# FFN output projection of a hybrid diffusion step as seven block products over the sample tokens

## The reference

```python
    x = x + g1 * (merged @ p['w_out'])
    h2 = _rmsnorm(x, p['norm2_g']) * (1 + sc2) + sh2
    gu = h2 @ p['w_ffn_in']
    gt, up = gu[..., :FFN_HIDDEN], gu[..., FFN_HIDDEN:]
    x = x + g2 * ((jax.nn.silu(gt) * up) @ p['w_ffn_out'])
```

## Time and profile before

| | us |
|---|---|
| median of 3 runs | 2460.69 (2458.73 to 2463.6) |
| profiled execution, its own time | 2461.89 |
| its span in the profile | 2460.1 |
| TensorE busy | 2360.2 (96%) |
| VectorE busy | 1184.8 (48%) |
| ScalarE busy | 782.5 (32%) |
| GpSimd busy | 167.3 (7%) |

### The profile page before, as it was taken

One profiled execution on the slowest core, in us unless ns is written; L12 is line 12 of the kernel. 1 busy time (PEld: TensorE's weight loads), 2 busy tenths in 40 slices (PEclk: granted clock), 3 DMA queues, 4 the chain that ended last, 5 costly groups with the idle time before them and its releaser, 6 DMA issues. The chain is left out here.

```text
span 2460.1 us, 44030 instructions
## 1 busy us (share of the span) xinstructions
PE 2360.2 (96%) x17899; PEld 2177.0 (88%) x17899; DVE 1184.8 (48%) x1912; ACT 782.5 (32%) x1284; POOL 167.3 (7%) x214
## 2 busy tenths in 40 slices
PE   7999999999999999989999999989999999999996
PEld 5887789999999898889999999878999999978775
DVE  5231111003554576645555558567665566435354
ACT  5311111113332233324444534233322232224332
POOL 0000000001100010112111010010000000001010
PEclk9999999999999999999999999999999999999998
DMA  6325532225542533123002075431222122156563
GB/s 269 120 109 187 178 109 100 83 73 190 169 167 96 170 108 115 59 77 131 26 17 90 9 300 170 120 86 54 80 80 71 62 80 80 49 207 205 191 213 118
DMA packets 120564, 296.31 MB, mean 120 GB/s; under 512 B 15440, under 2 KB 67360, under 8 KB 111088
## 3 DMA queue, kind: packets, MB, share of 16 engines
q1 hardware_dynamic: 81904, 217.43, 25.8%
q10 hardware_dynamic: 31536, 50.74, 5.6%
q0 software_dynamic: 6992, 26.22, 2.9%
HBM read 219.89 MB, written 74.52 MB: 120 GB/s over the span
## 5 line engine op out<-in xcount | busy, mean ns | idle before, releaser
L60 PE MATMUL ps<-mergedr,wt 128*128 128x512 f32 x1188 | 276.7, 395 | 16.7 <-DVE wt L2915 16.7
L60 PEld LDWEIGHTS ps<-mergedr,wt 128*128 128x128 f32 x1188 | 226.4, 191 | 66.7 <-DVE wt L2915 19.2
L60 PE MATMUL ps<-h_hi,fill_whi 128*128 128x384 f32 x672 | 235.4, 350 | 4.1 <-PEq L80 3.4
L60 PE MATMUL ps<-h_lo,fill_whi 128*128 128x384 f32 x672 | 226.2, 337 | 2.9 <-issue 2.9
L60 PE MATMUL ps<-h_hi,fill_wlo 128*128 128x384 f32 x672 | 226.6, 337 | 0.0
L60 PE MATMUL ps<-ys,mergedr 128*128 128x256 f32 (+1 forms) x1056 | 219.1, 296 | 0.9 <-DVE xb L2762 0.4
L60 PEld LDWEIGHTS ps<-ys,mergedr 128*128 128x128 f32 x1056 | 174.0, 190 | 1.3 <-issue 1.3
L60 PE MATMUL ps<-prj_whi,h_hi 128*128 128x512 f32 (+1 forms) x432 | 165.0, 382 | 4.4 <-DVE h_lo L624 4.4
L60 PE MATMUL ps<-prj_wlo,h_hi 128*128 128x512 f32 (+1 forms) x432 | 161.7, 374 | 0.0
L60 PE MATMUL ps<-prj_whi,h_lo 128*128 128x512 f32 (+1 forms) x432 | 161.5, 374 | 0.0
L60 PE MATMUL ps<-xb,mergedr 128*128 128x320 f32 (+1 forms) x528 | 156.5, 296 | 0.0
(11 more groups left out here) (404 smaller groups left out, 4790.9 us busy)
## 6 DMA issues: line engine op xcount, KB each, us to landing
wraw<-in_w_ffn_out SPq DMA_DIRECT2D x66, 512.0 KB, 3.5
wraw<-in_w_ffn_in SPq DMA_DIRECT2D x22, 1024.0 KB, 5.1
prj_raw<-in_w_ada SPq DMA_DIRECT2D x16, 1024.0 KB, 6.0
fill_raw<-in_w_fill SPq DMA_DIRECT2D x30, 512.0 KB, 4.2
bg_dram<-fill_st ACTq DMA_DIRECT2D x72, 192.0 KB, 2.0
xf<-bg_dram POOLq DMA_DIRECT2D x24, 576.0 KB, 7.6
wraw<-a_dram SPq DMA_DIRECT2D x66, 192.0 KB, 3.5
tok_dram<-prj_tst ACTq DMA_DIRECT2D x45, 256.0 KB, 2.1
```

The lines of the kernel that those rows point to most:

```text
L60: mm = pe.matmul(out, lhs[a], rhs[b], start=first and n == 0, stop=last and n == 2, skip_group_check=onto)
```

## The change

The FFN output projection becomes seven block products too, for the sample tokens. The sample tokens are split into two sets of 512 (of every tile of 128, the first 64 and the last 64), the hidden width into two halves of 11 blocks (`NP`), the output columns into two halves of 512. Each of the seven products is 11 units of 4 row tiles x 3 passes = 12 matmuls; the 128 context tokens are not in this scheme and ride along in the first two products (22 units) with 2 column halves x 3 passes = 6 matmuls more. `PRODUCTS` says for each product its operand in `a_dram`, its four PSUM banks, and whether it adds to what is there.

- The sums of activation halves are made on GpSimd: in `combine(p)`, once steps 2p and 2p+1 have given hidden blocks p and 11+p (the order of `w_ffn_in` is changed for that), four operations of 128x512. `store_sums(p)` stores the results; `a_dram` now holds seven operands.
- `w_ffn_out` is loaded once and stays in SBUF (`wrow`). GpSimd makes the four sums of its blocks (44 operations of 128x512: 11 during the first product, 22 behind them, 11 behind the context tile's `inverse`).
- Three sets of split operands (`u % 3`) and four raw activation buffers instead of two of each. Units of the first two products split 128x1024 of weights and 128x640 of activations, the others 128x512 of each.
- The sums over products are taken out of PSUM and gated by VectorE between units (`gate_in`, L3102, L3111 and L3120 of the changed kernel), residuals being added in the same step; `norm` is as before.
- All residual, gate and output transfers go over SyncE's queue; outputs and residuals in pieces of 64 rows.
- At the joint, the low parts of unit 0 stand before `up_first` of the last step and those of unit 1 before `gate_second`; SyncE loads units 0 and 1 and the first weight rows during the last step.
- Tokens stay in natural order: tiles of the second stage are plain tiles of 128, loaded and stored in one piece.
- All 77 units are written out, without loops.

```diff
+        PRODUCTS = ((0, X, False), (2, X, True), (1, Y, False), (3, X, False), (4, Y, False), (5, X, True), (6, Y, True))
+        NU = 7 * NP
...
+            def store_sums(p):
+                sp.wait_ge(s_done, 4 * p + 4)
+                sp.dma_start(g.a_dram[bass.ds((NP * 3 + p) * P, P), :], stage[0][1]).then_inc(a_out[0], 16)
+                for n, x in ((4, s1_buf), (1, s2_buf), (6, s4_buf)):
+                    sp.dma_start(g.a_dram[bass.ds((NP * n + p) * P, P), 64:HT], x).then_inc(s_out, 16)
...
+            def operand(u):
+                n, p = divmod(u, NP)
+                at, k = PRODUCTS[n][0], k_in[u % 4]
+                if u >= 4:
+                    sp.wait_ge(k_lo, 2 * u - 6)
...
+            weight_row(0)
+            operand(0)
+            weight_row(1)
+            sp.wait_ge(mm, 14 * L + 6)
+            operand(1)
+            weight_row(2)
+            weight_row(3)
+            sp.wait_ge(mm, 14 * L + 10)
+            for r in (4, 5, 6):
+                weight_row(r)
+            store_a(2, NP - 1, 0, 1, 4 * L + 2)
+            sp.wait_ge(mm, 14 * NH)
+            operand(2)
+            operand(3)
+            store_a(5, NP - 1, 1, 1, 4 * L + 4)
+            for u in range(4, NU):
+                operand(u)
+                if u + 3 < 2 * NP:
+                    weight_row(u + 3)
+                if u == 5:
+                    store_sums(NP - 1)
+                if u == 7:
+                    sp.dma_start(g2p, g.gate_rows[0, D:2 * D].partition_broadcast(P)).then_inc(c_in, 16)
...
+            def combine(p, more=True):
+                gp.wait_ge(a_done, 8 * p + 8)
+                if more:
+                    gp.wait_ge(s_out, 48 * p)
+                gp.tensor_tensor(s1_buf, second, fourth, ALU.add).then_inc(s_done, 1)
+                gp.wait_ge(s_done, 4 * p + 1)
+                gp.tensor_tensor(second, first, second, ALU.subtract).then_inc(s_done, 1)
+                gp.tensor_tensor(s2_buf, s1_buf, first, ALU.subtract).then_inc(s_done, 1)
+                gp.wait_ge(s_done, 4 * p + 3)
+                gp.tensor_tensor(s4_buf, third, s2_buf, ALU.subtract).then_inc(s_done, 1)
+
+            combine(0, False)
+            with gp.Fori(0, NP - 1) as i:
+                combine(i + 1)
...
+            for p in range(NP):
+                gp.wait_ge(k_lo, 2 * p + 1)
+                low, up = wrow[p][:, 0:BL], wrow[p][:, BL:D]
+                gp.tensor_tensor(low, up, low, ALU.subtract).then_inc(t_done, 1)
+            for p in range(NP):
+                r = NP + p
+                gp.wait_ge(row_in[r % 8], 16 * (r // 8) + 16)
+                gp.wait_ge(mm, 14 * NH)
+                gp.wait_ge(t_done, p + 1)
+                low, up, other = wrow[p][:, 0:BL], wrow[p][:, BL:D], wrow[r][:, BL:D]
+                gp.tensor_tensor(t2_w[p], other, low, ALU.subtract).then_inc(t_done, 1)
+                gp.tensor_tensor(up, other, up, ALU.subtract).then_inc(t_done, 1)
+            inverse(CX, 1, 2, 2 * CX + 1)
+            for p in range(NP):
+                low = wrow[NP + p][:, 0:BL]
+                gp.wait_ge(k_lo, 2 * (NP + p) + 1)
+                gp.wait_ge(t_done, NP + 2 * p + 1)
+                gp.tensor_tensor(low, low, t2_w[p], ALU.subtract).then_inc(t_done, 1)
...
+            def operand_hi(u):
+                n, p = divmod(u, NP)
+                e, wide_w, lo = u % 3, D if n < 2 else BL, 0 if n < 2 else 2
+                if u >= 3:
+                    act.wait_ge(k_mm, u - 2)
+                if n < 2:
+                    act.wait_ge(row_in[u % 8], 16 * (u // 8) + 16)
+                elif sums_of(u):
+                    act.wait_ge(t_done, sums_of(u))
+                act.activation(o_w[e][0][:, 0:wide_w], raw_weight(u), ACT.Copy).then_inc(k_hi, 1)
+                act.wait_ge(k_in[u % 4], loads_of(u))
+                act.activation(in_units(a_w[e][0])[:, lo:, :], raw_operand(u)[:, lo:, :], ACT.Copy).then_inc(k_hi, 1)
...
                 up_second(j, 1, 14 * j + 10)
                 lo(4)
+                if not more:
+                    operand_lo(0)
+                if s:
+                    v.wait_ge(s_done, 2 * j)
                 v.wait_ge(a_out[1 - s], 16 * j - 16 * (1 - s))
                 up_first(j, 0, 14 * j + 11, 1 - s)
                 up_first(j, 1, 14 * j + 12, 1 - s)
                 lo(5)
+                if not more:
+                    operand_lo(1)
                 gate_second(j, 0, 14 * j + 13, 1 - s)
                 gate_second(j, 1, 14 * j + 14, 1 - s)
-
...
+                if 24 <= u < 28:
+                    r = u - 24
+                    v.wait_ge(low_in, 128)
+                    v.wait_ge(k_mm, 2 * NP)
+                    gate_in(r, 0, ps[:, X[r], :], g2, 3 + r, 3 + r)
+                if u == 32:
...
+            for u in range(NU - 3):
+                unit(u)
+            for r in range(4):
+                for u in range(NU - 3, NU):
+                    if r == 0:
+                        pe.wait_ge(k_lo, 2 * u + 2)
+                    ins = rows(u, r, False, u == NU - 1, True)
+                ins.then_inc(last_mm, 1)
```

More of the change, by code:

```diff
@@ L29 @@
 HT = T // 2
+AW = HT + 64
 HEADS = 4
@@ L37 @@
 NH = FFN // P
+NP = NH // 2
 EPS = 1e-6
@@ L2247, in tail, with loads_of, sums_of @@
+        def loads_of(u):
+            return sum(32 if i < 2 * NP else 16 for i in range(u % 4, u + 1, 4))
+        def sums_of(u):
+            n, p = divmod(u, NP)
+            return {2: NP + 2 * p + 1, 3: NP + 2 * p + 2, 4: p + 1, 5: 3 * NP + p + 1}.get(n, 0)
         ss, ms, rstd = (ph.sb(n, [P, NT]) for n in ("ss", "ms", "rstd"))
+        sq = ph.sb("sq", [P, 2 * NT])
         half = ph.sb("half", [P, 1])
@@ L2359, in _ @@
             load_w(2, 0)
[L2360 removed]
+            store_a(0, 0, 0, 0, 2)
             with sp.Fori(0, 9) as i:
[L2362 to L2377 removed]
+                load_w(2 * i + 3, 1)
+                store_a(2, i, 0, 1, 8 * i + 6)
+                store_a(5, i, 1, 1, 8 * i + 8)
+                store_sums(i)
+                load_w(2 * i + 4, 0)
+                store_a(0, i + 1, 0, 0, 8 * i + 10)
@@ L2397, in _ @@
+            for i in (4, 5, 6, 7):
+                put_y(i, i - 2)
+            for i in range(4):
+                put_y(i, i + 6)
+            sp.wait_ge(y_out, 32 * NT)
         @block.gpsimd
@@ L2440, in _ @@
-            for n in range(3):
-                gp.wait_ge(y_out[n], 48)
+            first, second = (stage[0][a][:, 64:HT] for a in range(2))
+            third, fourth = (stage[1][a][:, 64:HT] for a in range(2))
+            def combine(p, more=True):
[8 more added lines that the diff above has]
+                gp.tensor_tensor(s4_buf, third, s2_buf, ALU.subtract).then_inc(s_done, 1)
@@ L2443, in _ @@
+            inverse(CX, 1, 2, 2 * CX + 1)
[5 more added lines that the diff above has]
+            for r in range(4):
+                inverse(4 + r, 6 + r, 11 + r, 2 * (4 + r))
+            for r in range(4):
+                inverse(r, 2 + r, 15 + r, 2 * r + 1)
         @block.scalar
@@ L2972, in _, with last @@
+            def last(r):
+                v.wait_ge(last_mm, r + 1)
+                gate_in(r, 1, ps[:, Y[r], :], g2, 23 + r, 23 + r)
+            last(0)
+            last(1)
+            norm(0, 6)
+            last(2)
+            norm(1, 7)
+            last(3)
+            norm(2, 8)
+            norm(3, 9)
         @block.tensor
@@ L3107, in _, with rows @@
-            for n in range(3):
-                for c in range(2):
-                    for e in range(2):
-                        ins = rows(2, n, e, False, e == 1, range(c, c + 1))
-                ins.then_inc(tile_mm, 1)
+            def rows(u, r, start=False, stop=False, onto=False, bank=None, cols=0):
+                e, lo = u % 3, 128 + 128 * r
+                return three_passes(pe, ps[:, PRODUCTS[u // NP][1][r] if bank is None else bank, :],
+                                    [x[:, lo:lo + P] for x in a_w[e]], [x[:, cols:cols + BL] for x in o_w[e]],
+                                    start, stop, onto)
@@ new lines, in context, with unit @@
+            def context(u):
+                for c in range(2):
+                    ins = rows(u, -1, u == 0, u == 2 * NP - 1, False, 6 + c, BL * c)
+                return ins
+            FREE_X = {1: (p1_kept, 1), 2: None, 3: (took, 3), 4: (took, 7), 5: (took, 11), 6: (took, 15)}
+            def unit(u):
+                n, p = divmod(u, NP)
+                onto = PRODUCTS[n][2]
+                pe.wait_ge(k_lo, 2 * u + 2)
+                if u == 0:
+                    pe.wait_ge(gate_done, 2 * NH)
+                    pe.wait_ge(u1_done, 2 * NH)
+                if n == 1:
+                    ins = context(u)
+                    if p == NP - 1:
+                        ins.then_inc(ctx_mm, 1)
+                for r in range(4):
+                    if p == 0 and FREE_X.get(n):
+                        sem, at = FREE_X[n]
+                        pe.wait_ge(sem, at + r)
```

(11 more changed lines are left out.)

429 lines of the change are left out of this document (216 added, 213 removed).

## The result

The changed kernel takes 2408.16 us (median of 4 runs, 2405.4 to 2409.46), the kernel before 2461.66 beside it: ratio 0.9782, 95% interval 0.9765 to 0.9799, 53.5 us less. Forecast were 2413.4 us and 47.3 us less. The profiled execution took 2407.87 us, its span is 2406.1.

A forecast was written before the change was run, and what follows sets the result against it. TensorE was taken to bound the kernel everywhere. 2150.5 + 240.1 + 5 + 2 + 0.7 + 14.5 = 2412.8 us of span, 47.3 below 2460.1, gave a forecast time of 2413.4 us; range 2402 to 2428.

The forecast's parts named there:

- the rival in which GpSimd costs nothing: Output projection: turns only where both engines have work, lead of two units swallows them; 5 and 2 us fall away; chance 0.16.
- FFN input projection: Stage ahead of the output projection: GpSimd's `combine` sums delay nothing that reaches TensorE, 0 us; stage ends at 2150.5.
- Matmuls: Output projection: 1,056 matmuls instead of 1,188, at 0.2274 us each, 240.1 us, 30.1 less.
- The joint: From input to output projection: TensorE's first waits of 2.12 and 6.09 us go.
- Sums on GpSimd: Output projection: sums shut VectorE out by turns; waits about 1, 1 and 3 us in products one to three, together 5.
- Clock: Output projection: scattered short waits slow TensorE's clock, costing 2 us, between 0 and 6.
- The last units: Unit 76 at the end of the output projection: a TensorE wait of 0.7 us, instead of 2.96 and 1.8 of slow matmuls.
- The end: From last matmul to kernel end: 14.5 us instead of 16.2, gain 1.7, between 0 and 4.
- then 5.5: Kernel end: 5.5 us without work behind the last transfers, kept as in the kernel before.
- The chain up to the last norm: Last row tile behind the last matmul: `gate_in`, square, GpSimd's addition and power, `norm`; 5.9 us, against 6.7 before.
- the signs named: Output projection: matmul about 0.227 us, stretched low parts in units 11 to 33, L3029 waits 3 to 8 us; input projection 473.
- the rival about the weight load: FFN input projection: `load_w` falls behind `store_sums` and lands late; slower than before, 2475 at 5 us each; chance 0.02.

The follow-up runs named there:

- the two experiments that take the waits away: Changed kernel with 44 weight sums cut to 8 columns: 2404.62 us; changed kernel with five third-loop sums moved to units 41 to 45: 2404.14 us.

## Why the prediction was right, and where its terms were off

The mechanism was right in the main: fewer matmuls at the same price, the waits of the joint and of the pass changes gone, a small price for sums. The result lies 5.2 us under the forecast and 2.2 above the 2406 of the rival in which GpSimd costs nothing, so by the time alone the rival was nearer. All terms but the first were put too high or just right, so the range was not hit by errors that cancel. The working in the span's terms, forecast 2412.8, measured 2406.1:

- *FFN input projection*, 2150.5 forecast, 2151.3 measured. Its length is the same 473 us; the difference lies ahead of it. `combine` at nothing: shown by cutting it short. The reason given holds as well: the gap ahead of `second_sum` shrank and never closed (0.49 us in the step of the earlier trace rows), and TensorE never waits there.
- *Matmuls*, 240.1: 1,056 at 0.2267 (4.08 us for 18) are 239.4.
- *The joint*, no wait, as forecast. That the order of the low parts takes the first wait away is shown by putting them back (2.38). That the loads at 2150 made most of the 6.09 is shown by moving them (1.60 is left). That it is gone because of more buffers, and the waits of the pass changes with it, is argued from that experiment and from the trace; no run has the new kernel with two buffers.
- *Sums on GpSimd*, 5 forecast, 2.4 measured in the stretch of the three waits, 1.7 to 2.8 in the two experiments that take the waits away. This is the term that was mis-sized. The first two products were put at 1 us each and cost nothing: a sum shuts VectorE out for 1.10 us, not 1.22, so a unit with two sums is 2.23 + 1.83 = 4.06 and not 4.3, just inside TensorE's 4.08. The third product was put at 3 and cost the 2.4. The rival "turns are taken only where both have work, and the lead swallows them" is refuted as a mechanism by the experiment with ten more sums, for which it says 0 and which cost 5.5 us, and by the steps of 4.05 us without the context matmuls. Its time was closer than mine all the same, since it dropped the clock term, rightly, and the end was too high in both.
- *Clock*, 2 forecast, 0 measured: granted clock 1.00 in every window of the stage. The waits of 0.4 us cost as much again in lost overlap, and nothing lasting.
- *The last units*, 0.7 forecast, 0.69 measured.
- *The end*, 14.5 forecast, 11.5 measured: the largest miss, 3.0 of the 6.7 us. The step that failed is "then 5.5": I took the empty stretch behind the last byte as fixed. It is 1.7 on SyncE's queue and 3.9 on GpSimd's, and the change moves the outputs from one to the other, which I had in the list of the change and did not price. The chain up to the last norm, 5.9 forecast, took 6.04; issue and transfers 3.8 instead of 2.4 to 3.1.

The measured terms add up to 2405.3; the 0.8 us that are missing lie in the stage, half of them in the overlap lost at the wait of 0.69 and in the end of the last matmul, the rest is not assigned. Of the signs named, the matmuls' price, the place of the stretched low parts, the name of the waits (L3029) and the 473 us came out; "3 to 8 us together" for the waits did not, they are 1.2 us. In the rival about the weight load 2420 + 10 x 6 is 2480 and not 2475; nothing hangs on it.

The Trainium skill's rule from "SBUF — State Buffer", section "Who interferes with whom", that such a pair of instructions excludes the other for its whole length, agrees with the rows shown (1.70 us for a pair, 0.60 alone), and it holds for a GpSimd operation of one column too (1.48 instead of 0.55). The estimate of 1.12 us for a sum from "GPSIMD Engine Reference", section "Elementwise — side-by-side cycle accounting", was nearer the truth than the 1.22 that I took: the runs show 1.10.

## What to carry to other kernels

Where two engines take turns, add their work per unit and compare the sum with what the bounding engine needs for that unit, stage by stage: below it the sharing is free, above it every unit pays once the lead is spent, and work without a due time can be moved to units that have room. A kernel at such a balance gives little back when the bounding engine is relieved: here taking away 25.8 us of matmuls bought 2 to 3.5 us, and 13 to 15 with the sums cut short too, the rest being held by transfers. And read the stretch behind the last byte as part of the price of the queue that issues the output.

## What had not been expected of the hardware

- In the stretches shown, VectorE's operations with both inputs in SBUF and GpSimd's sums alternate strictly, one instruction each: pairs of 1.70 us (512 columns), and 2.23 us for a low part of 1,024 columns with a sum. VectorE's operations with an input in PSUM took no turn (1.27 us for two beside a sum).
- Behind TensorE's waits of 0.4 us the granted clock stayed at 1.00, and so it did behind waits of 2.12 and 2.46 us in the kernel before and of 2.38 with the old order at the joint. Behind 2.60 us (ten sums more) it was 0.64, and 12 matmuls took 1.6 us more; behind 2.96 and 3.05 us in the kernel before it was 0.64 and 0.63. The length of the wait does not decide alone: with context and sums cut, 2.45 us were followed by 1.00 and 2.32 us, some 12 us behind a wait of 5.31, by 0.66.
- The same two stores cost 2.9 us more at the end of the kernel, from the last norm on, when GpSimd issued them than when SyncE did, 2.2 of them behind the last byte (one trace of each).
- Six loads of another queue delayed an operand's by several us in both places where they stood (ScalarE waited 12.85 us at the joint, 7.17 where they came later).
